# Compression pages requested in two transfers, one per group of heads, in a hybrid decoder step

## What is computed

```python
DEC_BATCH, PAST_LEN, PAGE_SIZE, N_KV, HEAD_DIM = 8, 1024, 128, 2, 64
L_CMP, STRIDE = 32, 16
# cache_k_cmp, cache_v_cmp: (1, 80, PAGE_SIZE, N_KV, HEAD_DIM); page_table: (8, 8) int32

def compress(k_full, w1, w2, cmp_pos):          # k_full (B, T, G, dk) -> (B, G, n_c, dk)
    lhs = k_full.transpose(0, 2, 1, 3).reshape(B * G, T, dk)
    w_blk = w1.reshape(L_CMP, HEAD_DIM, HEAD_DIM)
    h = lax.conv_general_dilated(lhs, w_blk, (STRIDE,), 'VALID', ...)
    h = h + jnp.einsum('ld,ldh->h', cmp_pos, w_blk)
    return (jax.nn.gelu(h) @ w2).reshape(B, G, h.shape[1], dk)

kc_cmp = compress(concat([gather_pages(cache_k_cmp), k_c]), w_phi_k1, w_phi_k2, cmp_pos)
vc_cmp = compress(concat([gather_pages(cache_v_cmp), v_c]), w_phi_v1, w_phi_v2, cmp_pos)
```

## Time and profile before

| what | value |
|---|---|
| median of 3 runs | 1399.03 us (1395.25 to 1399.77) |
| the profiled execution | 1397.42 us, its span 1395.8 us |
| TensorE matmul / weight load busy | 1300.6 us (93%) / 1200.5 us (86%) |
| VectorE / ScalarE / GpSimd busy | 565.1 us (40%) / 425.5 us (30%) / 184.3 us (13%) |
| chain that ended last | TensorE 85%, VectorE 7%, ScalarE 3% |
| mean granted TensorE clock | 0.964 of full speed |
| moved by DMA | 156.09 MB in 253199 packets |

### The profile page before, as it was taken

How to read it: one execution, slowest core, us unless ns; L and a number is a source line. 1 busy time by engine, 2 the same in 40 slices (tenths; PEclk the granted TensorE clock), 3 DMA queues, 4 the chain that set the end, 5 groups by cost and what they waited for, 6 DMA issues and landing times.

```text
span 1395.8 us, 26583 instructions
## 1 busy us (share of the span) xinstructions
PE 1300.6 (93%) x10210; PEld 1200.5 (86%) x10210; DVE 565.1 (40%) x962; ACT 425.5 (30%) x678; POOL 184.3 (13%) x351
## 2 busy tenths in 40 slices
PE   4999999999999997998858898979999999999996
PEld 3899999999999997995536566979999999999995
DVE  2422232222333356114457776584332333233355
ACT  2222222222211134225435655243222222211123
POOL 3000000000000026543071052033000000000020
PEclk9899999999999998999969999989999999999996
DMA  9545455454544345842523045212323232222211
GB/s 293 170 123 167 133 151 149 132 169 120 174 117 126 100 93 117 189 114 76 190 60 93 1 135 139 88 50 61 90 75 90 75 90 76 87 70 83 83 55 68
DMA packets 253199, 156.09 MB, mean 112 GB/s; under 512 B 46187, under 2 KB 247159, under 8 KB 253063
## 3 DMA queue, kind: packets, MB, share of 16 engines
q1 hardware_dynamic: 247759, 139.83, 35.6%
q0 software_dynamic: 5376, 15.43, 3.8%
HBM read 150.86 MB, written 8.60 MB: 114 GB/s over the span
## 4 chain that ended last, share of the span: by engine, by line
PE 85%; DVE 7%; ACT 3%; DVEq 2%; issue 1%; DMA 1%; SPq 0%; POOL 0%; POOLq 0%; ACTq 0%
PE ps L307 68%; PE ps L776 3%; PE ps L1967 2%; PE ps L1166 2%; DVE AR L2000 1%; PE ps L785 1%; PE ps L284 1%; ACT AR L1385 1%; DVE XT L470 1%; PE ps L1183 1%; PE ps L1156 1%; PE ps L1265 1%; DVEq L469 1%; PE ps L369 1%; DMA AR<-in_x_sample_dram 1%
## 5 line engine op out<-in xcount | busy, mean ns | idle before, releaser
L307 PE MATMUL ps<-UH,WH 128*128 128x288 f32 x1680 | 361.1, 296 | 3.1 <-ACT MU L641 1.6
L267 DVE TENSOR_TENSOR WL<-RAW,WH 128x1024 fp32r<-128x1024 f32 x159 | 197.1, 1240 | 408.0 <-ACT WH L263 402.8
L307 PE MATMUL ps<-UH,WL 128*128 128x288 f32 x1680 | 357.7, 294 | 0.0
L307 PE MATMUL ps<-UL,WH 128*128 128x288 f32 x1680 | 357.6, 294 | 0.0
L307 PEld LDWEIGHTS ps<-UH,WH 128*128 128x128 f32 x1680 | 268.4, 188 | 3.6 <-ACT MU L641 1.8
L307 PEld LDWEIGHTS ps<-UL,WH 128*128 128x128 f32 x1680 | 269.6, 187 | 0.0
L307 PEld LDWEIGHTS ps<-UH,WL 128*128 128x128 f32 x1680 | 268.6, 188 | 0.0
L263 ACT ACTIVATE WH<-RAW 128x1024 fp32r<-128x1024 f32 x159 | 167.2, 1052 | 211.6 <-PE ps L307 202.8
L307 PE MATMUL ps<-HH,WH 128*128 128x288 f32 x704 | 152.3, 297 | 2.9 <-DVE HL L658 2.7
L506 POOL TENSOR_TENSOR AR<-AR 128x576 f32<-128x576 f32 x18 | 29.5, 1639 | 933.8 <-ACT AR L417 874.8
L307 PE MATMUL ps<-HH,WL 128*128 128x288 f32 x704 | 150.8, 295 | 0.0
(11 more groups left out here) (309 smaller groups left out, 1281.0 us busy)
## 6 DMA issues: line engine op xcount, KB each, us to landing
RAW<-in_w_ffn_in_dram SPq DMA_DIRECT2D x88, 512.0 KB, 5.0
AW<-in_w_ada_dram SPq DMA_DIRECT2D x56, 512.0 KB, 4.3
RAW<-in_w_ffn_out_dram SPq DMA_DIRECT2D x32, 448.0 KB, 3.7
RAW<-in_w_ffn_out_dram SPq DMA_DIRECT2D x16, 512.0 KB, 3.9
AR<-in_w_ada_dram SPq DMA_DIRECT2D x7, 1024.0 KB, 11.1
RAW<-in_w_in_dram SPq DMA_DIRECT2D x28, 256.0 KB, 3.8
AR<-in_cache_k_cmp_dram POOLq DMA_DIRECT2D x64, 64.0 KB, 2.6
AR<-in_cache_k_slc_dram SPq DMA_DIRECT2D x64, 64.0 KB, 2.7
```

What stands on the lines that cost most here:

```text
L267: nc.vector.tensor_tensor(WL[:, slot, :], RAW[:, slot, :], WH[:, slot, :].bitcast(F32), ALU.subtract).then_inc(split_done, 1)
L307: mm = nc.tensor.matmul(ps[:, 2 * uslot + h, 0:HT], W[:, wslot, k * P:(k + 1) * P], R[:, k0 + k, h * HT:(h + 1) * HT], start=(first and k ...
```

## The change

The layout of a page in `PG` becomes (group, parity, number) along the free side instead of (parity, group, number). To get it, each page is requested in two transfers, one for each group: 64 partitions, two pieces of 256 B each. All 128 pages are so fetched by 256 requests. A transposed bank then holds one group, with (parity, number) on the partitions as `KT8` wants it, and one operation of 128 partitions copies it: ScalarE takes group 0, VectorE group 1. The counts that TensorE waits for double with the requests. Transposes and convolutions keep number and size.

```diff
         def page_load(eng, kv, b, j, full, page):
-            eng.dma_start(PG[64 * (j % 2):64 * (j % 2) + 64, ds(b + NB * kv, 1), j // 2, :],
-                          (cache_k_cmp, cache_v_cmp)[kv][0, ds(page, 1)].rearrange("a (t q) g d -> (a t) (q g d)", q=2)
-                          ).then_inc(full, 16)
+            for g in range(NG):
+                eng.dma_start(PG[64 * (j % 2):64 * (j % 2) + 64, ds(b + NB * kv, 1), j // 2, g * P:(g + 1) * P],
+                              (cache_k_cmp, cache_v_cmp)[kv][0, ds(page, 1), :, g:g + 1].rearrange("a (t q) g d -> (a t) q (g d)", q=2)
+                              ).then_inc(full, 16)
@@ turn_pages
-                pe.wait_ge(kpg_full, 16 * NB * NPG)
+                pe.wait_ge(kpg_full, 32 * NB * NPG)
-                pe.wait_ge(vpg_full, 16 * 2 * NPG)
-                pe.wait_ge(vpg_sp, 16 * (NB - 2) * NPG)
+                pe.wait_ge(vpg_full, 32 * 2 * NPG)
+                pe.wait_ge(vpg_sp, 32 * (NB - 2) * NPG)
-                for q in range(2):
+                for g in range(NG):
                     for j in range(4):
-                        mm = nc.tensor.transpose(ps[:, 2 * (b % 2) + q, j * P:(j + 1) * P], PG[:, n, j, q * P:(q + 1) * P],
+                        mm = nc.tensor.transpose(ps[:, 2 * (b % 2) + g, j * P:(j + 1) * P], PG[:, n, j, g * P:(g + 1) * P],
                                                  IDN[:, :])
-        def compress_evac(eng, kv, q):
+        def compress_evac(eng, kv, g):
-                for g in range(NG):
-                    dst = KT8[64 * q:64 * q + 64, g, b]
-                    src = ps[64 * g:64 * g + 64, 2 * (b % 2) + q, :].rearrange("p (j l) -> p l j", l=8)
-                    if q == 0:
-                        ev = nc.scalar.activation(dst, src, ACT.Copy)
-                    else:
-                        ev = nc.vector.tensor_copy(dst, src)
-                ev.then_inc((kt_a, kt_d)[q], 1)
+                src = ps[:, 2 * (b % 2) + g, :].rearrange("p (j l) -> p l j", l=8)
+                if g == 0:
+                    nc.scalar.activation(KT8[:, g, b], src, ACT.Copy).then_inc(kt_a, 1)
+                else:
+                    nc.vector.tensor_copy(KT8[:, g, b], src).then_inc(kt_d, 1)
```

## The result

The changed kernel takes 1423.42 us (median of 4 runs, 1421.9 to 1424.46). The kernel before, run beside it, takes 1398.36 us. The ratio is 1.0181, with a 95% interval of 1.016 to 1.0202: slower by 25 us. The forecast was 1416 us, slower by 17, with a range of 1406 to 1429. The time lies within the range and the sign was right, but the size was short by a third, and the queue that was to cost the time was the wrong one, as the following lines show.

What follows compares the result with a forecast made beforehand. TensorE's `w_in` products and VectorE's copies in the turns were taken to bound the kernel. Key delay 22.6, copies -7.2 and clock 1.5 sum to 16.9 us, giving 1416 us, range 1406 to 1429.

Steps and rivals of the forecast that it cites:

- the copies: Key and value turns: full-height copies take 0.69 us on VectorE, 0.6 on ScalarE; 3.6 us saved a turn, -7.2 us for both.
- GpSimd's term: Key page requests doubled on GpSimd: last issued at 647.7 us, keys complete at 653.6, delaying the key turn by 22.6 us.
- parallel delays count once: SyncE's and GpSimd's delays before the key turn run at the same time; the later, 22.6 us, counts, not their sum.
- SyncE's requests (doubled), values: Value requests between weight loads in `w_in`: rounds of 16.9 to 17.1 us, product 14 ending at about 643.5, hidden behind the keys.
- dear case: SyncE's value requests at 0.77 us each: product 14 of `w_in` would end at 649 us.
- the slack: SyncE's weight chunks in `w_in`: 5.4 us of lateness are free before a product has to wait.
- the tables: Stores now fall on the load of the reversed bias tables, awaited at line 1357; put at nothing, 0 to 6 us in the range.
- rival 4: GpSimd's late duties reach the path, by stores meeting table loads or late value pages: 6 us more, 1422; chance 0.12.
- The clock: Idle time before the key turn lowers TensorE's granted clock, slowing the first transposes: +1.5 us (0 to 5).
- Rivals 1 and 2: Page requests nearly free to issue, 1392 us, chance 0.06; or partly hidden, say 0.45 us each, 1399 us, chance 0.04.
- Rival 3: Pieces of 256 B block the DMA queues and weight loads land late: 13 us more, 1429 us; chance 0.09.
- Rival 5: In the turns, a full-height strided copy takes as long as two halves: +22.6 + 1.5, 1423 us; chance 0.03.

Runs made afterwards that it cites:

- e1: Changed kernel with only the key pages in two requests and the new copies, values as in the kernel before; ratio to the kernel before 1.0146.
- e2: Changed kernel with only the value pages in two requests and the new copies, keys as in the kernel before; ratio to the kernel before 1.0199.
- e9: Changed kernel with the DRAM-to-DRAM state copies issued behind the store of line 1002; ratio to the kernel before 1.0153.
- e7: Kernel before with only values in two requests, SyncE's spread behind weight chunks, loops written out; 1394.07 us against 1396.75, ratio 0.9974.
- e10: Changed kernel, keys and values shared out anew over GpSimd and SyncE, state copies behind line 1002; 1395.56 us against 1397.64 before, ratio 0.9992.
- e8: Changed kernel, page requests spread, 56 of SyncE's behind the last weight chunk, state copies in the first FFN; ratio to the kernel before 1.0221.
- e5: Changed kernel with the DRAM-to-DRAM state copies moved into the first FFN; ratio to the kernel before 1.0226.
- e4: Changed kernel with each copy of 128 partitions cut into two of 64; ratio to the kernel before 1.0212.
- e6: Kernel before with only the DRAM-to-DRAM state copies moved into the first FFN; ratio to the kernel before 1.0061.

## Why the prediction was right and wrong

**Right: the copies.** 0.69 and 0.60 us for 128 partitions, turns of 8.7 us, 7.9 us saved (7.2 predicted). **Right: GpSimd's term.** 0.597 us a request, 0.64 us apart within a sixteen, last key request at 649.7 (predicted 651.0); e1 shows 21.3 us of idle time for the 22.6 predicted. **Right: parallel delays count once.** e1 and e2 together with the changed kernel show it.

**Wrong: the step "SyncE's requests (doubled), values".** It gave a round of 16.9 to 17.1 us and the end of `w_in` at 643.5, with 649 for its dear case; measured were 18.9 us and 656.1. The lateness of SyncE's last group of weight requests is 628.00 - 598.84 + 0.8 (for the earlier start) = 30.0 us: 4.3 us were there already at the group of 551.13 (547.64 before), and four rounds of 19.2 us in place of 12.8 add 25.7. TensorE's products end 26.6 us late, 1.7 of it from their own duration, so 5.1 us were absorbed. That is the slack that the prediction had worked out, 5.4. The rest of the step was short three times:
- The count of rounds. "One's excess goes into the slack; three remain" left out that the two blocks of pages before 547 us would make SyncE late too. They used up nearly all of the slack, and four rounds came in full. TensorE's pauses are thus four, of 4.3 us in the mean (4 was predicted), but the first begins at 572.6 and not at 583. By the predicted round (4.3 us of excess) this gives 4.3 + 4 x 4.3 - 5.4 = 16.1 us, an end at 646.
- The price of a page request. With two pieces a partition it takes SyncE 0.559 us, one every 0.77, not 0.71: sixteen hold it for 12.4 us, not 11.2. I took the spacing of the old form and put the dear one in brackets.
- The weight requests. With the page numbers left out, 2.7 us of the predicted round were for them and what lies between; it is 3.5 (median 0.589 us each in 553 to 628 us, 0.408 in 547 to 630 us before), and the first round took longer still. They land in 4.7 us, not 3.8. I took them as fixed.

Beyond these, the last three products took 20.85 us, not 3 x 6.36 = 19.1: the granted clock was 0.92 from 635 to 656 us, and the first matmuls behind the pause ran slower. Of the 13.4 us that the step was short (26.6 for 13.2), the count of rounds explains 2.9, the page requests 4 x 1.2 = 4.8, the rest of the four rounds 3.7, the last products 1.7 and the slack 0.3.

So the sum's form was right (the later of two delays, less 7.2), and the wrong one of the two was put in: 643.5 and 653.6 should have been 656.1 and 652.5. The forecast of 9 to 10 us of idle time before the turn is false for the same reason: there was 0.77 us, and the pauses lay in `w_in`. That 1423 us still lies in the range is in part luck. The term for the keys, 22.6 us, was not what cost the time, but it stood near the 26.6 us of the term that did, and covered half of the error: for the values alone (e2) the same working would have put the delay at 13.2 us, where 27.2 were measured.

**Partly wrong: the tables, put at 0.** The prediction's range of 0 to 6 us holds the 5.9 us that the trace shows between the end of the convolution and the taking of its result, and the chance of 0.12 for rival 4 was too small for a transfer that had 4 us of margin and was about to meet 4 MB. Its price at the end is about 4 us by the ratio of e9, within the noise. **The clock** (+1.5): not before the turn, where there was no pause. It was granted 0.74 in the stretches with pauses in `w_in`, and 0.50 from 717 to 732 us, behind the wait for the tables (1.00 from 693 to 699 us before). There line 1128 took 3.65 us instead of 1.93, and line 1137 7.1 instead of 5.6: all its 64 products at some 397 ns, where in the kernel before a part took 272.

**Rivals.** Rivals 1 and 2 fell: no request of this form took under 0.55 us. Rival 3 is not seen: from 545 to 650 us the DMA engines were 59% busy, 62 of 105 us, where 59 were predicted (37,373 packets and not 47,000, as the profile shows GpSimd's as pieces of 1 KB in the mean), and in e7 all value pages came in the same pieces of 256 B without any delay of `w_in`. Rival 5 fell with the 0.69 us. The sum over the terms as measured: 26.6 late, less 7.9, plus 5.4 for the tables (line 1128 starts 7.3 us after the convolution's end, for 1.9 before), plus 1.9 for lines 1128 and 1130 and 1.5 for line 1137 at the lower clock, less 1.5 for the steps of VectorE and ScalarE behind line 1137, which took 9.4 us for 10.9. That is 26.0 us; A + C differ by 26.1 (222.0 - 195.9), the medians by 25.1.

## What to carry to other kernels

When requests are added to a queue between the loads on which a loop lives, compare the queue's whole round with the consumer's: here 11.2 us against 12.7 was hidden, 18.9 against 12.7 costs over 6 us every round, and a copy saved elsewhere can't repay it. Where two queues get later, compute both to the end and take the later, with the dear price for each, since the errors of both sums decide which one it is. For the values, the same layout costs nothing if its requests lie where the queue has cover (e7); for keys and values together no gain could be told (e10). Look at what stands behind them in that queue's program (e8) and at which loads the shifted transfers will meet (e5, e9).

## What the runs showed of the hardware

- The time for which a request holds its engine depends on its form, on SyncE above all: 325 ns for 32 rows of 1 KB, 491 for 64 rows of 1 KB, 559 for 64 rows of two pieces of 256 B; on GpSimd 496, 522 and 597 ns. A constant place in SBUF changed nothing (558 ns). What in the form sets SyncE's price stays open.
- Two DMAs of 2 MB from DRAM to DRAM delayed other queues' loads: the tables landed in 16.7 us instead of 7.7 (7.8 again in e9, with the copies moved away), `w_pool` (256 KB) in 11.1 us in the kernel before and 16.7 in e4 instead of 4.0, and one weight load of 512 KB made ScalarE wait 11.3 us (e6).
- SyncE's weight requests grew from 0.408 to 0.541 us (medians, 547 to 630 us) with twice as many page requests between them. In e7, where the loop was written out, they took 0.591 us, and TensorE's products had no gap: while they are hidden, dearer requests show nowhere. Why they grew stays open.
- Behind pauses of 3.3 to 6 us TensorE's matmuls in `w_in` started slower: a pair of 128x288 took 0.68 us where it takes 0.42 at full clock (granted clock 0.51 from 578.57 to 584.6 us, 0.77 from 597.4 to 604.8).
